# First attention of a two-block transformer kernel: queries and keys in split halves stacked on the array's rows, the gate term summed by the tensor engine, the mask added in PSUM

## The reference, cut to what matters

```
cum    = cumsum(log_f)                                  # per head, over the 512 tokens
logits = q . k / sqrt(64) + (cum[query] - cum[key])     # for keys up to the end of the 128-query block
logits = where(query >= key, logits, -inf)
y_att  = softmax(logits) @ v
```

## Time and profile before

| | |
|---|---|
| Median of 3 runs | 1467.79 us (1466.78 to 1469.92) |
| The profiled execution, time | 1472.37 us |
| The profiled execution, span | 1470.6 us |
| Mean granted clock of TensorE | 0.992 |
| PE busy | 1421.8 us (97%), 6751 instructions |
| DVE, ACT, POOL busy | 696.7, 520.9, 655.5 us |
| PE's share of the chain that ended last | 89% |
| The 18 steps of the first attention | from 263.3 us to 466.9 us of the span |

### The profile page before, as it was taken

The page is one execution under the profiler, slowest core; times in us unless marked ns, Lnnn a source line. Parts: engine busy times, 40 slices in busy tenths (PEclk is TensorE's granted clock), DMA queues, the critical chain, the costliest instruction groups (busy, mean ns, idle before and its releaser), DMA issues.

```text
span 1470.6 us, 17517 instructions
## 1 busy us (share of the span) xinstructions
PE 1421.8 (97%) x6751; PEld 1169.5 (80%) x6751; DVE 696.7 (47%) x1023; ACT 520.9 (35%) x744; POOL 655.5 (45%) x512
## 2 busy tenths in 40 slices
PE   2999999999999989999999997999999999999999
PEld 2887788778788878888888886887788888888887
DVE  6677954488862766131223637427613213132131
ACT  0635433334444454132231425324435313232231
POOL 1543445434231855545445554761144454454452
PEclk9999999999999999999999999999999999999999
DMA  9353245353523342232232322221012322323222
GB/s 330 106 145 86 86 143 183 104 172 129 165 79 115 112 120 86 89 106 90 87 113 86 98 102 86 86 86 58 30 62 83 115 86 90 109 86 114 86 87 85
DMA packets 119991, 157.38 MB, mean 107 GB/s; under 512 B 5196, under 2 KB 81248, under 8 KB 119936
## 3 DMA queue, kind: packets, MB, share of 16 engines
q1 hardware_dynamic: 117744, 151.15, 32.0%
q0 software_dynamic: 1648, 5.39, 1.1%
...
HBM read 154.45 MB, written 2.17 MB: 107 GB/s over the span
## 4 chain that ended last, share of the span: by engine, by line
PE 89%; DVE 5%; POOL 3%; ACT 1%; issue 1%; DMA 1%; SPq 0%; DVEq 0%; ACTq 0%; POOLq 0%
PE bank L1474 26%; PE bank L1476 25%; PE bank L1475 25%; PE bank L1619 3%; PE bank L1814 2%; POOL w_lo L490 2%; PE bank L1609 2%; DVE tmp L1052 1%; PE bank L1940 1%; PE bank L1734 1%; PE bank L1594 1%; DMA arena<-in_w_ada_dram 1%; PE bank L1584 1%; ACT w_hi L623 0%; POOL head_rs L469 0%
## 5 line engine op out<-in xcount | busy, mean ns | idle before, releaser
L490 POOL TENSOR_TENSOR w_lo<-raw,w_hi 128x512 fp32r<-128x512 f32 x428 | 586.5, 1401 | 625.9 <-ACT w_hi L623 624.8
L1474 PE MATMUL bank<-w_hi,a_hi 128*128 128x512 f32 x928 | 364.1, 392 | 8.7 <-DVE a_lo L963 6.0
L1475 PE MATMUL bank<-w_lo,a_hi 128*128 128x512 f32 x928 | 361.9, 390 | 0.0
L1476 PE MATMUL bank<-w_hi,a_lo 128*128 128x512 f32 x928 | 361.7, 390 | 0.0
L623 ACT ACTIVATE w_hi<-raw 128x2048 fp32r<-128x2048 f32 x107 | 204.7, 1913 | 354.2 <-PE bank L1476 350.6
L1474 PE MATMUL bank<-a_hi,w_hi 128*128 128x512 f32 x800 | 317.3, 397 | 3.1 <-DVE a_lo L963 2.2
L1475 PE MATMUL bank<-a_lo,w_hi 128*128 128x512 f32 x800 | 314.0, 393 | 0.0
L1476 PE MATMUL bank<-a_hi,w_lo 128*128 128x512 f32 x800 | 313.9, 392 | 0.0
L1474 PEld LDWEIGHTS bank<-w_hi,a_hi 128*128 128x128 f32 x928 | 174.6, 188 | 46.4 <-DVE a_lo L963 6.2
L1476 PEld LDWEIGHTS bank<-w_hi,a_lo 128*128 128x128 f32 x928 | 174.6, 188 | 36.5
L1475 PEld LDWEIGHTS bank<-w_lo,a_hi 128*128 128x128 f32 x928 | 174.7, 188 | 35.7
...
## 6 DMA issues: line engine op xcount, KB each, us to landing
...
```

The source lines that it names most:

```text
L490: last = pool.tensor_tensor(w_lo[:, u0 % 2, cols], raw[:, u0 % 2, cols], w_hi[:, u0 % 2, cols].bitcast(F32), ALU.subtract)
L1474: pe.matmul(out_, hi_a, hi_b, start=start, stop=False)
L1475: pe.matmul(out_, hi_a, lo_b, start=False, stop=False)
L1476: return pe.matmul(out_, lo_a, hi_b, start=False, stop=stop)
```

## The change

- `q_split` and `k_split` hold, for two pairs of heads, four float32r operands of 128 rows each. For a head: `hh` has hi(q) on all 128 rows (the same 64 rows twice); `lh` has lo(k) on the head's own 64 rows and hi(k) on the other 64; `l1` has lo(q) on its own rows and ones on the others; `hc` has hi(k) on its own rows, and on the others two rows with the high part and the rest of `-cum[key]`, and zeros. Two matmuls into the same place, `hh` by `lh` and `l1` by `hc`, then give hi.lo + hi.hi + lo.hi and the gate term. The scores of a head are eight float32r matmuls on 128 rows instead of four float32 ones on 64.
- ACT splits with four activations of 64 rows for each query or key tile (`split_hi`, one copy before), DVE with two subtractions (`split_lo`, none before).
- DVE adds only the mask, in PSUM, to the diagonal blocks (three instructions instead of seven), and takes the maxima from PSUM; ACT's exponentials read PSUM. `prob` has one buffer. The next scores wait for the exponentials (`p_made`) instead of `s_made`.
- POOL writes the constant halves once (`constant_halves`: four copies and four multiplications of 64x512 that stand ahead of the `w_lo` of the first query and key unit), splits the gate rows once (`save_rows`), and for each pair of heads issues two small DMAs that put the gate rows into `k_split` (`cum_rows`). Its addition per head and SP's broadcast row per head are gone.
- A weight unit of queries and keys holds one pair's queries and keys and is loaded in two DMAs.
- Half of v's second 512 columns moves into steps 0 and 1; the query and key tiles stand in steps 2 to 13; `wo1_half(2, 0)` and `(2, 1)` move behind the steps. The `late_columns` are spread: one behind each v half and in chosen steps (`LATE_STEP`); six `late_ada` stand ahead of DVE's steps, four before. In DVE's step `output` is now last, not first.

```diff
+V_BANKS = ((4, 5), (0, 1))
 N3_BANKS = (4, 5, 6, 7, 4, 5, 6, 7)
-WO1_HALF = {12: (0, 0), 13: (0, 1), 14: (1, 0), 15: (1, 1), 16: (2, 0), 17: (2, 1)}
+WO1_HALF = {14: (0, 0), 15: (0, 1), 16: (1, 0), 17: (1, 1)}
+LATE_FIRST = 6
+LATE_STEP = (1, 2, 3, 5, 6, 7, 9, 10, 11, 13)
...
-        ncb = view(8192, 2, S)
-        ncm = view(9216, 2, S)
-        qk = view(14336, 2, 4, S)
-        prob = view(18432, 2, 1280)
+        prob = view(18432, 1280)
...
+        def q_pair(p, half):
+            return q_split[:, p % 2, half], q_split[:, p % 2, 2 + half]
+        def k_pair(p, half):
+            return k_split[:, min(p, 1), half], k_split[:, min(p, 1), 2 + half]
+        def own(half):
+            return slice(HD * half, HD * half + HD)
+        def other(half):
+            return slice(HD - HD * half, P - HD * half)
...
+            def qk_pair(u, p):
+                if u >= 3:
+                    sp.wait_ge(w_lo_made, u - 1)
+                for side, col in enumerate((C_Q, C_K)):
+                    sp.dma_start(raw[:, u % 2].rearrange("p (k s n) -> p k s n", k=8, s=2)[:, :, side],
+                                 w_in_v[:, :, col + P * p:col + P * p + P]).then_inc(landed[u % 2], 16)
...
             def save_rows():
                 pool.wait_ge(scanned, 5)
                 pool.dma_start(acs_d, dtf[0:16, 1, :]).then_inc(acs_out, 16)
-                pool.dma_start(ncum_d, dtf[32:48, 1, :]).then_inc(cum_out, 16)
+                hi_part, rest = dtf[32:48, 3, :], dtf[32:48, 4, :]
+                pool.wait_ge(w_lo_made, U_XBC + 5)
+                pool.tensor_copy(hi_part.bitcast(F32R), dtf[32:48, 1, :]).then_inc(cum_hi, 1)
+                pool.wait_ge(cum_hi, 1)
+                pool.tensor_tensor(rest.bitcast(F32R), dtf[32:48, 1, :], hi_part, ALU.subtract).then_inc(cum_hi, 1)
+                pool.wait_ge(cum_hi, 2)
+                pool.dma_start(ncum_d[0], hi_part.bitcast(F32R)).then_inc(cum_out, 16)
+                pool.dma_start(ncum_d[1], rest.bitcast(F32R)).then_inc(cum_out, 16)
+            def cum_rows(pair):
+                if pair >= 2:
+                    pool.wait_ge(s_mm, 2 * pair)
+                for half in range(2):
+                    hc, _ = k_pair(pair, half)
+                    o = HD - HD * half
+                    pool.dma_start(hc[o:o + 2], ncum_d[:, 2 * pair + half, :]).then_inc(cum_in[pair % 2], 16)
+            def constant_halves():
+                pool.wait_ge(ada_sum, 4)
+                pool.wait_ge(xs_made, 10)
+                pool.wait_ge(cb_done, 2)
+                pool.wait_ge(w_lo_made, U_QK)
+                for half in range(2):
+                    for n in range(2):
+                        one = ones[other(half), :].unsqueeze(1).broadcast_to([HD, TB, P])
+                        pool.tensor_copy(q_pair(n, half)[1][other(half)].rearrange("p (a b) -> p a b", a=TB), one).then_inc(ones_set, 1)
+                        pool.wait_ge(ones_set, 2 * half + n + 1)
+                        pool.tensor_scalar(k_pair(n, half)[0][other(half)].rearrange("p (a b) -> p a b", a=TB), one, 0.0, None, ALU.mult)                            .then_inc(zeros_set, 1)
+                        pool.wait_ge(zeros_set, 2 * half + n + 1)
...
-            for u in range(U_Z, U_V + 4):
+            for u in range(U_Z, U_QK):
                 lo(u)
+            constant_halves()
+            for u in range(U_QK, U_V + 4):
+                lo(u)
+                if u == U_V:
+                    pool.wait_ge(cum_out, 32)
+                    cum_rows(0)
+                    cum_rows(1)
             rms_root(0, RMS_EPS)
-            ...
+            for u in range(U_QK1, U_WO1 + 4):
+                lo(u)
+                if u == U_QK1 + 1:
                     relative()
+                if U_QK1 + 1 <= u < U_WO1 + 1:
+                    cum_rows(u - U_QK1 + 1)
...
-            def qk_tile(g, j, u, b):
-                ...
+            def split_hi(n, b):
+                pair = n // 2
+                act.wait_ge(ticks, 2 * unit_of(n) + n % 2 + 1)
+                if pair >= 2:
+                    act.wait_ge(s_mm, 2 * pair if n % 2 else 2 * pair - 2)
+                for half in range(2):
+                    first, second = (k_pair if n % 2 else q_pair)(pair, half)
+                    if n % 2 == 0:
+                        second = first
+                    for dst in (first[own(half)], second[other(half)]):
+                        act.activation(dst, bank[b][own(half), :], ACT.Copy, scale=1.0 if n % 2 else HD ** -0.5).then_inc(qk_hi, 1)
...
             for s in range(18):
                 ...
                 if s >= 2:
                     copy_probT(s - 2, probT)
...
+                    probabilities(s - 1, score, prob)
+                if s % 2 == 0 and 2 <= s < 14:
+                    hi(U_QK1 + s // 2)
+                elif s == 17:
                     hi(U_WO1 + 2, late=1)
+            hi(U_WO1 + 3)
+            wo1_tile(2)
+            wo1_tile(3)
...
-            def fox_scores(h):
-                ...
+            def split_lo(n, b):
+                for half in range(2):
+                    rows_ = own(half)
+                    dve.wait_ge(qk_hi, 4 * n + 2 * half + 2)
+                    if n % 2:
+                        hc, lh = k_pair(n // 2, half)
+                        dve.tensor_tensor(lh[rows_], bank[b][rows_, :], hc[rows_].bitcast(F32), ALU.subtract).then_inc(qk_lo, 1)
+                    else:
+                        hh, l1 = q_pair(n // 2, half)
+                        dve.scalar_tensor_tensor(l1[rows_], bank[b][rows_, :], HD ** -0.5, hh[rows_].bitcast(F32),
+                                                 ALU.mult, ALU.subtract).then_inc(qk_lo, 1)
+            def fox_maxima(h):
                 dve.wait_ge(s_mm, h + 1)
-                ...
-                dve.wait_ge(s_made, h + 1)
-                maxima(h, lambda q: prob[:, h % 2, QO[q]:QO[q] + (q + 1) * P])
+                for b, o, n in ((4, 256, 2), (6, 128, 1), (5, 384, 1)):
+                    diagonal = bank[b][:, o:o + n * P].rearrange("p (a k) -> p a k", a=n)
+                    last = dve.tensor_tensor(diagonal, diagonal, hide.unsqueeze(1).broadcast_to([P, n, P]), ALU.add)
+                link(last)
+                maxima(h, lambda q: bank[SB[q][0]][:, SB[q][1]:SB[q][1] + (q + 1) * P])
...
             ssd()
-            split_turned(T_SSM, 1, lambda k: v0[:, V_SSM + k:V_SSM + k + 1], SSM_BANKS)
-            for n in range(4):
+            for n in range(2):
+                split_lo(n, 6 + n)
+            for half in range(2):
+                split_turned(T_SSM + 4 * half, 1, lambda k: v0[:, V_SSM + 4 * half + k:V_SSM + 4 * half + k + 1],
+                             SSM_BANKS[4 * half:4 * half + 4], 4 * half)
+                split_lo(2 + half, 6 + half)
+            for n in range(LATE_FIRST):
                 late_ada(n)
             for s in range(18):
+                if 1 <= s < 17:
+                    fox_maxima(s - 1)
+                if 3 <= s < 15:
+                    split_lo(s + 1, (s - 1) % 2)
+                if s in LATE_STEP:
+                    late_ada(LATE_FIRST + LATE_STEP.index(s))
+                elif s == 16:
+                    late_mod()
                 if s >= 2:
                     h = s - 2
                     output(h, att[:, :, h * HD:h * HD + HD])
-                if s < 16:
-                    fox_scores(s)
-                if s < 12:
-                    late_ada(4 + s)
-                elif s == 15:
-                    late_mod()
...
+            def v_half(d, b):
+                ...
+            def fox_scores(h):
+                pair, half = h // 2, h % 2
+                if half == 0:
+                    pe.wait_ge(cum_in[pair % 2], 32 * (pair // 2 + 1))
+                    pe.wait_ge(qk_lo, 4 * pair + 4)
+                hh, l1 = q_pair(pair, half)
+                hc, lh = k_pair(pair, half)
+                for q in range(TB):
+                    b, o = SB[q]
+                    rows_, n = slice(P * q, P * q + P), (q + 1) * P
+                    pe.matmul(bank[b][:, o:o + n], hh[:, rows_], lh[:, 0:n], start=True, stop=False)
+                    last = pe.matmul(bank[b][:, o:o + n], l1[:, rows_], hc[:, 0:n], start=False, stop=True)
+                last.then_inc(s_mm, 1)
...
-            row_pair(U_V, 0, N_V[0], 0)
-            pe.wait_ge(qk_read, 4)
-            row_pair(U_V + 2, 1, N_V[1], 0)
+            row_half(U_V, 0, 0, 0, 0, True, False)
+            pe.wait_ge(qk_lo, 8)
+            late_columns(0)
+            row_half(U_V, 1, 0, 0, 4, False, True)
+            late_columns(1)
+            v_half(2, 0)
+            late_columns(2)
+            v_half(2, 1)
+            late_columns(3)
             pe.wait_ge(evac[0], 4 * (N_V[0] + 1))
-            def filler_free(n):
-                if n >= 2:
-                    pe.wait_ge(qk_read, 4 + n - 1)
             for s in range(18):
                 if s >= 2:
```

(26 more changed lines are left out.)

178 lines of the change are left out of this document (72 added, 106 removed).

## The result

The changed kernel takes 1454.3 us (median of 4 runs, 1450.9 to 1456.05) against 1468.9 us (4 runs, 1466.8 to 1472.2): ratio 0.9893, 95% interval 0.9874 to 0.9913. That is 14.6 us less; 17.6 us less and a time of 1450 us were forecast. Of the 4.3 us between 1450 and 1454.3, 3.0 are the smaller gain. Another 1.1 are the kernel before, which was that much slower here than in the three runs that the forecast started from. The rest is rounding. The profiled execution has a span of 1451.1 us against 1470.6 us.

The account below looks back on a forecast made before the run. PE's work was taken to bound the kernel, DVE next. Terms 16.8 + 3.4 + 2.1 - 0.5 - 2.0 - 2.2 = 17.6 us, against 1467.8 us, gave 1450 us; range 1444 to 1460 us.

Parts of the forecast that it names:

- scores, 16 heads: PE's scores fall from 2.35 to 1.30 us a head with float32r: 16.8 us gained (bounds 0 and 19.2).
- long steps: Four stalls of 0.53 us at the last transposes, behind DVE's output, go: 2.1 us gained (bounds 2.1 and -3).
- new wait in step 1: PE waits for the exponentials ahead of the next scores, cover thin in step 1: 0.5 us lost (bounds 0 and 3).
- constant halves: POOL's eight new instructions delay DVE in the SSD chunks through shared SBUF ports: 2 us lost (bounds 0 and 7).
- end of the steps: wo1_half(2, 0) and (2, 1) back to back wait on rounding, splits and bank copies: 2.2 us lost (bounds 0.5 and 4).
- clock: The slow-clock stretch behind step 0's sixteen one-column sums goes as sums are spread: 3.4 us gained (bounds 0 and 3.4).
- as worked out: The forecast's main case, all terms as summed: 1445 to 1454 us, chance 0.60.
- rival 1: DVE and POOL costs at their far ends: 1462 us, or 1456 at half; band 1454 to 1463, chance 0.24.
- signs of being right: Scores 1.2 to 1.35 us, 10.5 us steps, clock 1.00 from 200 us, no long steps, last SSD products 1-4 us late.
- Rival 2: In the scores, short float32r matmuls are no cheaper than float32: 1458 us at half way, 1467 in full; chance 0.08.
- Rivals 1 and 3: DVE and POOL costs at their far ends (chance 0.24); the scores' single buffer becoming the bound, 1475 us (chance 0.05).

Follow-up runs that it names:

- rows64: Changed kernel with one float32 product over the head's own 64 rows per score block, not two float32r over 128 rows; 1472.4 us (1.0022 of before).
- sums_row: Changed kernel with eight more one-column sums (sixteen instructions) in a row just ahead of the first scores; 1459.6 us (0.9936 of before).
- w_hi_early: Changed kernel with ACT's w_hi of the even steps ahead of the exponentials instead of behind them; 1454.9 us (0.9918 of before).
- constants_late: Changed kernel with POOL's eight constant-half instructions moved from 160 to 175 us to its pause beginning at 195.5 us; 1453.1 us (0.9894 of before).
- three_moves: Changed kernel with v's last eighths reordered, one late_ada load earlier, constant_halves() behind lo(U_V), wo1's copies 2 and 3 first; 1455.3 us (0.9906 of before).

## Why the prediction held, step by step

| term | forecast, us | measured, us | from |
|---|---|---|---|
| scores, 16 heads | 16.8 | 15.2 | 2.35 - 1.40 = 0.95 each |
| transposes behind them | none | 2.4 | 1.24 - 1.09 = 0.15 each |
| long steps | 2.1 | 2.1 | all gone |
| new wait in step 1 | -0.5 | 0 | none there |
| wait for `w_lo` in the v phase | none | -2.5 | waits |
| constant halves | -2.0 | -0.9 | 36.18 - 35.27 |
| end of the steps | -2.2 | -1.7 | waits: 1.4 + 0.3 |
| sum without the clock | 14.2 | 14.6 | 14.1 by the runs |
| clock | 3.4 | 1.1 | mean over runs, not clear of zero; 5.1 in the two profiles up to the end of the steps |

rows64 splits the 14.1 us otherwise: 18.3 us from the scores and their transposes (17.6 in the table) and -4.2 us from all the rest without the clock (-3.0 in the table). So about 1 us of cost has no row of its own here.

The measured 1454.3 us lies in the stated range, and the main term, by itself larger than the whole gain, is right in mechanism. The rest is in part luck. The sum without the clock was 14.2 us and the runs give 14.1, but it comes out through errors of -1.6, +2.4, +0.5, -2.5, +1.1 and +0.5 us that cancel. The time is also 0.3 us above the band called "as worked out" (1445 to 1454) and inside that of rival 1, though rival 1's causes did not come.

Of the signs of being right, the steps of 10.5 us without a gap and the end of the long steps came. The scores, at 1.40 us, are above the 1.2 to 1.35 us. The clock is not 1.00 from 200 us on. The last SSD products start at 187.3 us, not 1 to 4 us later than 187.6: they are 0.9 us late counted from those of chunk 1, but chunk 1 came 1.2 us earlier in this execution (151.14 against 152.36).

- **The scores.** Right, and a little off in the price: a 128-column float32r product takes 0.11 us only as the second of its pair, the first 0.17. The gain in the transposes was not in my sum; by rows64 it belongs to the 64-row products of before. The two errors nearly cancel. Rival 2 is out. One reading was wrong and did no harm: the four instructions of the earlier trace rows are two products in the program, not four, so a float32 product of 512 columns takes 1.72 / 2 = 0.86 us and not 0.43. The sum used only the float32r price and the 2.35 us of a whole head.
- **The clock.** This is the term that was mis-sized, and it accounts for 2.3 of the 3.0 us by which the gain fell short. I took one stretch of one execution as a property of the kernel. That execution was already 4.6 us above the median and lost 11.8 us to the clock against a mean of 9.5; I moved the base down to the median and still counted the whole stretch as gained. The stretch is gone, as forecast, and so is one at 190 us, but one at 250 us came in its place, and over the runs the kernels differ by 1.1 us. That the spread sums are what removed the stretch near 270 us is not shown, and sums_row does not decide it.
- **The long steps.** Gone for the reason given; w_hi_early brings three of them back by the order of `w_hi` alone.
- **The new wait.** Wrong in place. I looked for it in step 1, where the exponentials end at 268.15 us and PE comes to its sums at 268.46 and to the scores at 268.80: it does not have to wait, but the cover is 0.3 us. It is in the v phase, and it follows from the cut of v into halves: a weight unit must last 7.6 us of `w_hi` and `w_lo`, and a half lasts 5.5. I had priced the six loads behind the weight loads and not the units themselves. The bound of 3 us happened to hold it.
- **The constant halves.** The mechanism is right and the size half: five DVE instructions were lengthened by 0.3 to 0.4 us each, and not by a whole POOL instruction (0.6 us for the copy, 1.48 us for the multiplication, with nothing beside them). The Trainium skill ("SBUF — State Buffer", section "SBUF: two separate sides") describes an exclusive lock. By it a DVE instruction would wait for the POOL instruction in progress. Beside the constants the trace does not agree: in constants_late four DVE instructions that take 4.63 us by themselves and two pairs of POOL's that take 2 x (0.60 + 1.48) = 4.16 us ran within 6.4 us, so they overlapped, and in the sum the reading by whole instructions was too dear. Beside `w_lo` the trace can agree: the instruction of 6.12 us in three_moves was held until POOL had done. The measured delays decide for each neighbour.
- **The end of the steps.** Nearly as worked out: 0.5 us at the first copies, 0.9 at the second and 0.3 in step 14. `g_row` stands between `wo1_half(2, 0)` and `(2, 1)`, which I had overlooked; it covers the second unit's `w_lo`. Chain of waits at the first copies:

```profile
431.77 1.91 ACT w_hi L675
433.68 0.58 ACT arena L905
```

- **Rivals 1 and 3.** Neither came in its causes, but for the part of the clock that stayed lost. The exponentials end 6.1 us behind the scores (359.43 - 353.31; 5.9 worked out) and are needed at 8.9. DVE has room in the steps, 68% busy, except in step 14.
